# A hybrid encoder block on one core: seams and recurrent tiles in another order, and the layer norm's offset on VectorE

## The reference

```python
proj = x @ w_in            # attention q,k,v; DeltaNet q,k,v; beta, decay, z; two gates
y_attn = banded_sink_attention(rope(aq), rope(ak), av, sink)   # chunks of 64, window of 128
dq, dk, dv = split(silu(conv4(dqkv)));  dq, dk = l2norm(dq), l2norm(dk)
o = gated_delta_rule(dq, dk, dv, beta, g)   # per chunk of 64: (I + M)^-1, then a scan of a state
y_dn = rmsnorm(o) * dn_norm_w * silu(z)
merged = sig(gate_a) * (y_attn @ w_branch_attn) + sig(gate_b) * (y_dn @ w_branch_dn)
x = layer_norm(ALPHA * x + merged @ w_out, ln1_g, ln1_b)
h = square(relu(x @ w_up))                                     # 4096 wide
x = layer_norm(ALPHA * x + h @ w_down, ln2_g, ln2_b)
```

## Time and profile before

| | |
|---|---|
| median of 3 runs | 1477.19 us (1477.19 to 1478.68) |
| profiled execution, its own time | 1479.21 us |
| its span, first to last instruction | 1477.3 us |
| mean granted TensorE clock | 0.992 |
| busy: TensorE, VectorE, ScalarE, GpSimd | 1426.5, 920.7, 525.0, 326.6 us |
| moved by DMA | 194.92 MB |

### The profile page before, as it was taken

One profiled execution on the slowest core, in us unless ns is written; L12 is line 12 of the kernel. 1 busy time (PEld: TensorE's weight loads), 2 busy tenths in 40 slices (PEclk: granted clock), 3 DMA queues, 4 the chain that ended last, 5 costly groups with the idle time before them and its releaser, 6 DMA issues.

```text
span 1477.3 us, 22473 instructions
## 1 busy us (share of the span) xinstructions
PE 1426.5 (97%) x8570; PEld 1178.7 (80%) x8570; DVE 920.7 (62%) x1728; ACT 525.0 (36%) x1184; POOL 326.6 (22%) x345
## 2 busy tenths in 40 slices
PE   7999999999999999999998899999999999999996
PEld 7888887877887788778887777888888788888885
DVE  3655313476657676465618778666665577777778
ACT  3212212333232323243202334555554444444540
POOL 3666534134213422234723000000000000000000
PEclk9999999999999999999999999999999999999998
DMA  7123533441344232133451132434443966556422
GB/s 216 71 88 112 162 118 96 114 115 56 103 115 129 76 84 87 54 128 129 172 198 71 72 128 107 157 157 157 157 157 128 332 205 197 166 170 185 124 69 114
DMA packets 121007, 194.92 MB, mean 132 GB/s; under 512 B 27664, under 2 KB 67664, under 8 KB 118608
## 3 DMA queue, kind: packets, MB, share of 16 engines
q1 hardware_dynamic: 111984, 174.21, 36.1%
q10 hardware_dynamic: 8928, 19.40, 3.4%
HBM read 135.84 MB, written 57.74 MB: 131 GB/s over the span
## 4 chain that ended last, share of the span: by engine, by line
PE 89%; DVE 8%; issue 2%; ACT 1%; DMA 0%; SPq 0%; DVEq 0%; ACTq 0%
PE ps L1784 15%; PE ps L1719 8%; PE ps L1721 8%; PE ps L1720 8%; PE ps L2153 6%; PE ps L2155 6%; PE ps L2154 6%; PE ps L2134 6%; PE ps L2136 6%; PE ps L2135 5%; PE ps L1852 4%; PE ps L1792 2%; PE ps L1933 1%; PE ps L1730 1%; PE ps L1884 1%
## 5 line engine op out<-in xcount | busy, mean ns | idle before, releaser
L709 POOL TENSOR_TENSOR ring2l<-raw,ring2h 128x256 fp32r<-128x256 f32 x180 | 173.6, 995 | 3.6
L2153 PE MATMUL ps<-thi,shi 128*128 128x512 f32 x416 | 162.6, 391 | 2.6 <-DVE slow L1604 2.6
L2155 PE MATMUL ps<-thi,slow 128*128 128x512 f32 x416 | 162.5, 391 | 0.0
L2154 PE MATMUL ps<-tlow,shi 128*128 128x512 f32 x416 | 162.4, 390 | 0.0
L1784 PE MATMUL ps<-xh,ring2h 128*128 128x512 f32 x304 | 123.6, 407 | 0.1
L1784 PE MATMUL ps<-xl,ring2h 128*128 128x512 f32 x304 | 119.8, 394 | 0.0
L1784 PE MATMUL ps<-xh,ring2l 128*128 128x512 f32 x304 | 119.2, 392 | 0.0
L1719 PE MATMUL ps<-xh,ring2h 128*128 128x512 f32 x288 | 112.2, 390 | 0.0
L1720 PE MATMUL ps<-xl,ring2h 128*128 128x512 f32 x288 | 112.0, 389 | 0.0
L1721 PE MATMUL ps<-xh,ring2l 128*128 128x512 f32 x288 | 112.0, 389 | 0.0
L1611 DVE TENSOR_TENSOR tlow<-b,thi 128x512 fp32r<-128x512 f32 x104 | 71.9, 692 | 57.0 <-ACT thi L783 57.0
(11 more groups left out here) (350 smaller groups left out, 3263.3 us busy)
## 6 DMA issues: line engine op xcount, KB each, us to landing
raw<-in_wblk SPq DMA_DIRECT2D x55, 512.0 KB, 3.3
sraw<-hpark SPq DMA_DIRECT2D x104, 256.0 KB, 2.8
hpark<-hq SPq DMA_DIRECT2D x16, 1024.0 KB, 4.6
b<-in_wblk SPq DMA_DIRECT2D x64, 256.0 KB, 3.8
wraw<-in_wblk SPq DMA_DIRECT2D x30, 512.0 KB, 3.7
park<-ub ACTq DMA_DIRECT2D x50, 256.0 KB, 2.0
hpark<-hq SPq DMA_DIRECT2D x16, 768.0 KB, 4.8
park<-cout ACTq DMA_DIRECT2D x12, 512.0 KB, 2.6
```

What stands on the lines that cost most here:

```text
L709: ins = pool.tensor_tensor(lo[:, k:k + 2, :], src[:, k:k + 2, :], hi[:, k:k + 2, :].bitcast(F32), ALU.subtract)
L2153: mm(outp, shi[s][:, ts], thi[m][:, :], start=first, stop=False, skip_group_check=True)
L2154: mm(outp, shi[s][:, ts], tlow[m][:, :], start=False, stop=False, skip_group_check=True)
L2155: return mm(outp, slow[s][:, ts], thi[m][:, :], start=False, stop=final, skip_group_check=True)
```

## The change

Recurrent part: the three engines' lists of one step are reordered and the fill is cut otherwise. First seam: GpSimd's addition of ln1_b for tiles 0 to 3 goes away, VectorE adds it behind each multiplication; the transposes of tiles 0 to 3 stand behind `out_tile(4)` and `out_tile(5)`; the twelve standard up products run in the order `UORD`, first quarters of pairs 0 and 1 over tiles 0 to 3, then those over tiles 4 to 7; LayerNorm statistics of tiles 4 and 5, and of 6 and 7, are taken together; the sums for the seven-product form and the weights' splits change places. Second seam: four of the first six loads of h go out one product earlier, ahead of B11 (T1 and T2 swap places in SBUF, which frees the slots), and the first two steps' splits are taken earlier on ScalarE and VectorE. Renumbered waits (`hsq_ok`, `rl_ok` through `UORD`) are left out of the cut below.

```diff
-TX_KB = {"T1": 32, "T2": 48, "T4": 64, "T3": 80}
+TX_KB = {"T2": 32, "T1": 48, "T4": 64, "T3": 80}
...
-                    sp.wait_ge(up_mm, 4 * ((n - 4) // 2) + 3 + n % 2)
+                    sp.wait_ge(up_mm, UORD.index(((n - 4) // 2, 2 + n % 2)) + 1)
...
             last = 7 * (NP - N_STD - 1)
+            sp.wait_ge(sp_mm, last + U_P6)
+            for n in range(4):
+                load_s(n)
             sp.wait_ge(sp_mm, last + U_P4)
             for i in range(8):
                 load_down("B11", i, b11_in[0])
             sp.wait_ge(sp_mm, last + U_P5)
-            for n in range(NSR):
+            for n in range(4, NSR):
                 load_s(n)
             for i in range(8, NP):
                 load_down("B11", i, b11_in[1])
...
-            for t in range(4):
-                pool.wait_ge(g_ok, t + 1)
-                pool.tensor_tensor(acc[:, t, 1, :], acc[:, t, 1, :], lngb[:, 1, :], ALU.add).then_inc(x1_ok, 1)
...
                 if t is not None: b_ya(t, 0)
+                fill(0)
                 if t is not None: b_vn(t, 1)
+                if n is not None: a_scalars(n, 1 - p)
+                fill(1)
+                if t is not None: b_exps(t, 1)
                 if t is not None: b_osq(t)
-                fill(0)
-                if t is not None: b_exps(t, 1)
-                fill(1)
-                if n is not None: a_scalars(n, 1 - p)
                 if n is not None: a_eg(n)
+                if n is not None: a_squares_k(n)
+                fill(2)
                 if t is not None: b_pt(t, 1)
                 if n is not None: a_squares_q(n)
-                fill(2)
-                if n is not None: a_squares_k(n)
+                fill(3)
+                if t is not None: b_ya(t, 1)
                 if n is not None: a_exps(n)
-                if t is not None: b_ya(t, 1)
-                fill(3)
...
             for t in range(4):
                 norm(t)
+            for t in range(4):
+                x1_hi(t)
             norm(4)
             norm(5)
-            x1_hi(0)
-            x1_hi(1)
-            x1_hi(2)
-            up_split(0)
-            up_split(1)
-            x1_hi(3)
-            norm(6)
-            x1_hi(4)
-            norm(7)
+            for n in range(4):
+                up_split(n)
...
+            act.wait_ge(xp_out[0], 16 * 4)
+            up_out(0)
+            x1_hi(4)
+            x1_hi(5)
+            norm(6)
+            norm(7)
+            up_out(1)
+            up_out(2)
+            x1_hi(6)
+            x1_hi(7)
+            up_out(3)
+            up_out(4)
+            tx_his(0)
+            up_out(5)
+            up_split(4)
+            up_split(5)
+            for u in range(6, 9):
+                up_out(u)
+            tx_his(1)
+            up_out(9)
+            w_his(N_STD, 0, 7)
+            up_out(10)
+            up_out(11)
...
                 snap(q, U_P5, 2, Q_S2)
                 if q < NP - 1:
                     w_his(q + 1, 3, 7)
+                else:
+                    down_s(0)
+                    down_t(0)
                 snap(q, U_P1, 3, Q_S3)
+                if q == NP - 1:
+                    down_s(1)
+                    down_t(1)
...
                 if t is not None: b_max(t, 0, 1 - p)
                 if a is not None: a_m(a, p)
                 if t is not None: b_prob(t, 0)
+                if a is not None: a_qeg(a, p)
+                if a is not None: a_att(a, p)
                 if a is not None: a_ys(a, 1)
-                if a is not None: a_att(a, p)
                 if t is not None: b_state(t, 0, 1 - p)
                 if a is not None: a_tb(a, 1)
                 if a is not None: a_r(a, 1, p)
@@ -1385,25 +1395,24 @@
                 if a is not None: a_ys(a, 2)
                 if a is not None: a_tb(a, 2)
                 if a is not None: a_r(a, 2, p)
-                if a is not None: a_qeg(a, p)
+                if t is not None: b_max(t, 1, 1 - p)
                 if a is not None: a_ys(a, 3)
-                if t is not None: b_max(t, 1, 1 - p)
-                if t is not None: b_on(t, 1 - p)
+                if t is not None: b_state(t, 1, 1 - p)
                 if a is not None: a_tb(a, 3)
-                if t is not None: b_state(t, 1, 1 - p)
+                if a is not None: a_r(a, 3, p)
+                if n is not None: a_d(n, 1 - p)
+                if a is not None: a_ys(a, 4)
                 if t is not None: b_prob(t, 1)
-                if a is not None: a_r(a, 3, p)
-                if a is not None: a_ys(a, 4)
-                if n is not None: a_d(n, 1 - p)
                 if n is not None: a_em(n)
                 if a is not None: a_tb(a, 4)
                 if a is not None: a_r(a, 4, p)
+                if t is not None: b_on(t, 1 - p)
                 if a is not None: a_ys(a, 5)
-                if a is not None: a_r(a, 5, p)
-                if n is not None: a_kd(n, 1 - p)
                 if t is not None: b_yd(t)
                 if n is not None: a_norm(n, 1 - p)
+                if n is not None: a_kd(n, 1 - p)
                 if n is not None: a_vb(n, 1 - p)
+                if a is not None: a_r(a, 5, p)
...
             for t in range(4):
                 stats(t)
             deviation(0, 4)
-            for t in range(4):
...
-            for t in range(4, NT):
-                if t == 7:
-                    up_lo(0)
-                    up_lo(1)
-                combine(t)
-                if t == 6:
-                    x1_lo(1)
-                    x1_lo(2)
-                stats(t)
-                deviation(t, t + 1)
...
+            def place1(t):
                 scale1(t)
                 offset1(t)
 
+            for t in range(4):
+                place1(t)
+            combine(4)
+            x1_lo(0)
+            x1_lo(1)
+            stats(4)
+            combine(5)
+            x1_lo(2)
+            x1_lo(3)
+            stats(5)
+            deviation(4, 6)
+            place1(4)
+            place1(5)
+            combine(6)
+            stats(6)
+            up_lo(0)
+            up_lo(1)
+            combine(7)
+            stats(7)
+            up_lo(2)
+            up_lo(3)
+            deviation(6, 8)
+            x1_lo(4)
+            x1_lo(5)
+            place1(6)
+            place1(7)
+            x1_lo(6)
+            x1_lo(7)
...
-            for t in range(5, 8):
-                x1_lo(t)
-            up_lo(2)
-            up_lo(3)
             tx_sums(0)
-            up_sums(0)
             tx_los(0)
             up_lo(4)
             up_lo(5)
+            up_sums(0)
             tx_sums(1)
             up_sums(1)
             w_adds(N_STD)
-            tx_los(1)
-            w_los(N_STD)
+            for i in range(4):
+                tx_los(1, i, i + 1)
+                w_los(N_STD, i, i + 1)
+            w_los(N_STD, 4, 7)
             for q in range(N_STD, NP):
                 up_sums(q - 1)
                 if q < NP - 1:
                     w_adds(q + 1)
                     w_los(q + 1)
+                else:
+                    lo_s(0)
+                    lo_t(0)
                 up_quads(q)
-                if q == NP - 1:
-                    for n in range(2):
-                        lo_s(n)
-                        lo_t(n)
+            lo_s(1)
+            lo_t(1)
             up_sums(NP - 1)
             lo_s(2)
...
                 if t is not None: b_ks(t, 0, q)
                 if t is not None: b_scores(t, 0)
-                if a is not None: a_kq(a, p)
                 if a is not None: a_kk(a, p)
                 fill(f[1])
                 if a is not None: a_t1(a)
                 fill(f[2])
                 if t is not None: b_vn(t, 0, q)
-                if a is not None: a_y(a, 1, p)
+                if a is not None: a_kq(a, p)
                 fill(f[3])
                 if t is not None: b_pt(t, 0)
+                if a is not None: a_y(a, 1, p)
                 if t is not None: b_ds(t, 0, q)
+                if t is not None: b_pv(t, 0)
                 if a is not None: a_u(a, 1, p)
-                if t is not None: b_pv(t, 0)
                 fill(f[4])
+                if t is not None: b_scores(t, 1)
                 if t is not None: b_ks(t, 1, q)
-                if t is not None: b_o(t, 0, q)
                 if a is not None: a_y(a, 2, p)
                 fill(f[5])
-                if t is not None: b_vn(t, 1, q)
                 if a is not None: a_u(a, 2, p)
                 fill(f[6])
+                if t is not None: b_vn(t, 1, q)
+                if t is not None: b_o(t, 0, q)
+                if a is not None: a_y(a, 3, p)
+                fill(f[7])
                 if t is not None: b_ds(t, 1, q)
+                fill(f[8])
+                if a is not None: a_u(a, 3, p)
                 if t is not None: b_o(t, 1, q)
-                if a is not None: a_y(a, 3, p)
-                if t is not None: b_scores(t, 1)
-                if a is not None: a_u(a, 3, p)
```

(101 more changed lines are left out.)

30 lines of the change are left out of this document (9 added, 21 removed).

## The result

The changed kernel takes 1459.78 us in the median of 4 runs (1458.53 to 1461.35), the kernel before beside it 1477.93 (1477.19 to 1479.32): ratio 0.9877, 95% interval 0.9863 to 0.9891, 18.2 us less. The profiled execution has a span of 1458.6 us against 1477.3, 18.7 less, at the same mean clock of 0.992.

What follows compares the result with a forecast made beforehand. TensorE holds the span for 97%, so only its idle time and slow-clock stretches can be won back. Terms 9.1 + 12.5 - 2.7 = 18.9 us off 1477.2 give 1458.3 us; likeliest range 1454 to 1462, outer 1450 to 1467.

Steps and rivals of the forecast that it cites:

- the likeliest case's range: Whole kernel: time as the terms sum, 1454 to 1462 us, chance 0.55.
- Recurrence: 9.1 predicted: Recurrent steps: 1.15 us off each of 7 steps, 8.0, plus 0.5 first, 1.5 seventh, less 0.9 last.
- The places asked for: Recurrent step: when TensorE reaches each small product, e.g. a_y(4) at 32.2, a_u(4) at 34.2, a_y(5) at 39.6 us.
- Rival (3): Recurrence: GpSimd's rope holds up four operations, 3.0 us in each of 7 steps, 21 in all, 1479; chance 0.03.
- First seam: 12.5 predicted: Output to up projection: 17.0 us removed, 4.5 added by a new wait at the first two x1_t.
- Second seam: 2.7 lost predicted: Down projection's start: late eighth B11 block delays the seventh product; 6.9 us lost against 4.2 now.
- The third down step's wait of 2.3: Second seam: third down step waits for lows behind up_sums(15), 1167.2 against 1164.9, 2.3 us.
- (5): First seam's new wait: clock falls once more and reaches into work, 1.6 us more, 1460; chance 0.2, inside the range.
- the sign that the prediction named for being wrong: Whole kernel: more than two clock falls would show the forecast wrong.
- (1): Second seam won too: B11 lands in time, wait falls to 0.5 us; 6.4 less, 1452; chance 0.15.
- (2): Recurrence wins nothing: a_y(4) or a_u(4) late by 1.1 us a step, 1466; chance 0.25 with the first-seam-wait rival.
- (4): First seam keeps a 4 us wait at the fifth or eighth product, 1462 to 1463; 0.25 with the recurrence-wins-nothing rival.

Runs made afterwards that it cites:

- d_move: Kernel before with only two VectorE operations moved, a_tb(3) and a_r(3) ahead of the second chunk's b_on, b_state and b_prob: 1470.2 us, ratio 0.9944.
- best: Changed kernel with x1 transposes one output tile later, split semaphores for the first B11 blocks, and splits of down steps 2 and 3 ahead of up_sums(15): 1447.6 us.
- d_s1: Kernel before with the first seam's edits alone: 1469.3 us, ratio 0.9936.
- u_s2: Changed kernel with the second seam put back as it was before: 1457.3 us, ratio 0.9854.
- f_b11: Changed kernel with separate semaphores for B11 blocks 0, 1 and 2 to 7, same transfers in the same order: 1453.8 us, ratio 0.9837.
- f_b11r: Changed kernel with semaphores for B11 blocks 0, 1, 2 to 3, 4 to 7, and splits of down steps 2 and 3 ahead of up_sums(15): 1453.8 us.
- d_s2: Kernel before with the second seam's edits alone: 1481.0 us, ratio 1.0015.
- g_off: Changed kernel with the offset addition for tiles 0 to 3 moved back to GpSimd: 1462.7 us, ratio 0.9888.
- o_only: Kernel before with only the offset addition for tiles 0 to 3 moved from GpSimd to VectorE: 1478.5 us, ratio 0.9998.

## Why the prediction was right, step by step

The total was off by 1.5 us, inside the likeliest case's range; 0.7 of it is that the kernel before took 1477.9 us beside the changed one, not 1477.2. Two of the three terms were mis-sized, in opposite ways. That the traces differ by 18.7 us where the terms add up to 18.9 is partly luck: 0.8 of the 18.7 has no cause in the change, and misses of -1.9, +0.7 and +0.2 stand behind the rest.

**Recurrence: 9.1 predicted, 9.3 measured.** In a full step nothing waits, and the period is 46.21 against 46.33 (47.48 - 1.15): seven steps of 1.27 less are 8.9 where 8.0 were forecast. The rest brought 0.4 in place of 1.1; in the first step the waits came to 2.7 us after 2.6, so the 0.5 forecast there did not come. The places asked for hold within 0.3 us: the step's zero being 361.8, `a_y(4)` was put at 394.0, `a_u(4)` at 396.0, `a_y(5)` at 401.4:
```profile
394.11 0.68 PE L1875 MATMUL ps<-rinv,mm 64*64 64x64 f32 x16
...
396.08 0.68 PE L1875 MATMUL ps<-tb,ys 64*64 64x64 f32 x16
...
401.25 0.68 PE L1875 MATMUL ps<-rinv,mm 64*64 64x64 f32 x16
```
Rival (3), GpSimd's rope holding up what now stands beside it, did not come: rope starts at 382.49, 20.7 into the step, and beside its last part (386.75) `a_tb(2)` takes 0.42 as alone, while operations on 128x4 in SBUF still take 0.57 and 0.66 in place of 0.16 and 0.17:
```profile
386.88 0.42 DVE L1326 TENSOR_TENSOR tb<-tb,ps 128x256 f32<-128x256 f32 x1 [2.35 <-PE ps L1875]
...
388.41 0.57 DVE L1336 SCALAR_TENSOR_TENSOR mx<-smx,sink 128x4 f32<-128x4 f32 x1
389.01 0.66 DVE L1337 TENSOR_SCALAR nmx<-mx 128x4 f32<-128x4 f32 x1
```
That agrees with the rule of the Trainium skill (SBUF — State Buffer, Who interferes with whom) that the prediction weighed, for the operand from PSUM. The last row does not fit so well: it has one SBUF input and took 0.66 us all the same, which the rule allows in a two-port mode alone, and no run here shows the mode. `b_on`, the small chain, now runs at 397.8 to 401.6, after GpSimd is done. What the prediction did not see is how little of the reordering this takes (d_move).

**First seam: 12.5 predicted, 10.6 measured. The mis-sized term is the clock in the new wait.** The wait itself came as costed, 2.78 and 1.30 us against 2.9 and 1.6:
```profile
774.16 0.39 PE L1744 MATMUL ps<-slh,mg 128*128 128x512 f32 x1
777.33 1.09 PE L2102 MATMUL ps<-cst,acc 128*128 128x128 f32 x8 [2.78 <-DVE acc L1500]
779.72 1.97 PE L2102 MATMUL ps<-cst,acc 128*128 128x128 f32 x8 [1.30 <-DVE acc L1500]
781.35 0.78 PE L1742 MATMUL ps<-slh,mg 128*128 128x512 f32 x1
...
784.91 0.63 PE L1744 MATMUL ps<-slh,mg 128*128 128x512 f32 x1
```
The clock was costed at nothing there, 1.6 us at the most. But it falls in the second of the two waits and stays down into `out_tile(5)` (PEclk is the third number from the end):
```profile
778.00:780.00 2.00, 0.69 (x6) 0.46 (x5) 1.97 (x3) 1.11 (x3) 0.00 (x0) 0.76 0.68 266
780.00:782.00 2.00, 2.00 (x10) 1.91 (x10) 1.97 (x3) 0.87 (x2) 0.00 (x0) 0.50 0.66 260
782.00:784.00 2.00, 2.00 (x6) 1.58 (x5) 1.97 (x3) 0.33 (x1) 0.00 (x0) 0.50 0.57 231
784.00:786.00 2.00, 2.00 (x6) 1.55 (x5) 1.97 (x4) 0.00 (x0) 0.00 (x0) 0.54 0.45 182
```
B is 7.8 us above that of best: 4.4 of waits from start to start (2.94 and 1.47), and 3.4 of transposes and matmuls at 1.2 GHz, the lower of the clock's two levels (0.50 of 2.4 GHz in the windows). So 7.8 were added, not 4.5. The price is not fixed: five kernels with the same code there (changed, d_s1, u_s2, f_b11, f_b11r) lose 7.8, 7.2, 6.6, 6.2 and 6.8. On the other side more was removed than costed, 176.1 + 1.75 - 159.4 = 18.4 in place of 17.0, since the slow transposes and the 0.16 us from start to start around each wait were left out. The rule of the Trainium skill (TensorE: Matmul & The Clock Gate, Why this matters for your kernels) that the prediction set beside this sum, idle gaps make the clock drop, came out: the clock did fall once more, though the page speaks of longer gaps than either of these two, 2.78 and 1.30 us. The fall cost 3.4 us, twice the 1.6 that the prediction worked out for it from the old slow stretches. Those it had placed too early: in the kernel before the granted clock is still 1.00 in 810 to 811, 844 to 845 and 1158 to 1159 us and below it in the microsecond behind each, so the falls begin between 0.5 us before the end of their wait and 1.4 us behind it, not at 809, 843 or 1157. What the prediction said of all that follows held: no wait from there to 1130 us.

**Second seam: 2.7 lost predicted, 2.0 measured.** The mechanism is the one named. ScalarE stands at `down_t(0)` until the eighth block lands, and saves P1's bank behind it:
```profile
1126.92 0.62 ACT L784 ACTIVATE shi<-sraw 128x512 fp32r<-128x512 f32 x1
1134.10 0.63 ACT L784 ACTIVATE thi<-b 128x512 fp32r<-128x512 f32 x1 [6.55 <-DMA b<-in_wblk]
1134.63 0.58 ACT L784 ACTIVATE hq<-ps 128x512 f32<-128x512 f32 x1
```
The landing at 1134.1 is 1154.8 of the old time (seventh product without its wait at 1131.67 here, 1152.41 there), against 1155.0 forecast from the landings' spacing of 0.68. The wait is 3.53 (3.9 forecast). The third down step's wait of 2.3 did not appear; 2.3 us were lost in its place just ahead, at half clock:
```profile
1135.35 0.77 PE L2160 MATMUL ps<-x,slh 128*128 128x512 f32 x1 [3.53 <-ACT hq L784]
...
1140.18 0.63 PE L2162 MATMUL ps<-x,sll 128*128 128x512 f32 x1
```
First and last matmul lie 4.83 apart, against 2.50 in the earlier trace rows; with twelve slow matmuls TensorE came to the third step no sooner than its operands; with eight, in d_s2 and g_off, it waits 0.7 us there. So the clock cost 2.4 where 0.7 was costed, and the third step nothing where 2.3 was. C's 571.7 over best's 565.3, 6.5 before rounding, is close to the 6.9 forecast because the slow clock took the place of the wait: here the sum was right by two errors that cancel.

**Start: nothing predicted, 0.8 measured**, with no cause in the change: TensorE's wait for its first load is 7.6 us in the rows above, and in the kernel before
```profile
PE ps L1730 <- DMA xraw<-in_xT: 8.5, 1, 8.5
```
The terms: 9.3 + 10.6 - 2.0 + 0.8 = 18.7, against 9.1 + 12.5 - 2.7 = 18.9. Of the rivals, (5) is what happened inside the forecast: the fall reached into work. There were two falls in place of four, so the sign that the prediction named for being wrong, more than two, did not show. (1) was out of reach with the eight-block wait, and is what f_b11r makes of it. (2) and (4) found no wait.

## What to carry to other kernels

Look first at what stands ahead of a late operation in its own engine's list: two operations moved on VectorE gave four fifths of what three reordered lists and a new cut of the fill gave. A step placed earlier than its operands turns cover into a wait, and the wait is paid with the slow clock behind it on top, here 6.2 to 7.8 us in all for 3.2 to 4.1 of idle time; filling that wait with one more tile of ready work was worth more than the earlier start. And one semaphore for a batch of loads makes the first user pay for the last of them: splitting it won 6 us with the same transfers, 2.0 of which only make good what the second seam's edit had cost.

## What the runs showed of the hardware beyond the prediction

A fall of the clock can outlast the wait by far. In the kernel before some eight matmuls ran slow after one. In the changed kernel the windows above put it at half from about 779.0 to 785.8 us, though TensorE is at work again from 779.7, and all twelve matmuls behind the second seam's wait are slow. Behind waits of one length the loss differs from kernel to kernel, by one trace of each: after the same wait of 2.6 us at the first down product no matmul runs slow in o_only, 8 do in before and in d_s1, and 14 in u_s2; after the equal wait ahead of the seven-product form 8 are slow in before and none in d_move. Between the same two kernels, whose code is the same there, a fall also changed its place: before has 0.72 in 843 to 849 us, behind the wait of 2.4 us, and 1.00 in 880 to 886, behind that of 2.2; d_move has 1.00 in 836 to 842 and 0.72 in 870 to 876, behind the same two. What sets this was not tried. At 0.2 us for each slow matmul it makes a profiled span uncertain by 1.6 us (8) to 2.8 (14) at such a wait; best, which has none in that half, has no slow matmul there.
